# An RWKV-7 group inverse built from squares of 32 rows, with ScalarE copying the results of its last two levels

## The reference, cut to what matters

```
def wkv7_scan(r, w, k, v, a, b):        # a = -kk, b = kk * a
    # state S [64, 64] per head, one step for each token t:
    #   S_t = S_{t-1} * w_t + (S_{t-1} a_t) b_t^T + v_t k_t^T
    #   y_t = S_t r_t
```

## Time and profile before

| | us |
|---|---|
| median of 3 runs | 2042.83 (2038.61 to 2046.37) |
| the profiled execution | 2042.8 |
| its span in the trace | 2041.0 |
| four groups of the inverse (first fill of group 0 to last record of group 3) | 348.2 to 523.8 |
| a group with work of both neighbours beside it (392 to 438, 438 to 484) | 46.0 each |

### The profile page before, as it was taken

One profiled execution on the slowest core, in us unless ns is written; L12 is line 12 of the kernel. 1 busy time (PEld: TensorE's weight loads), 2 busy tenths in 40 slices (PEclk: granted clock), 3 DMA queues, 4 the chain that ended last, 5 costly groups with the idle time before them and its releaser, 6 DMA issues.

```text
span 2041.0 us, 44235 instructions
## 1 busy us (share of the span) xinstructions
PE 1972.0 (97%) x17620; PEld 1877.6 (92%) x17620; DVE 1070.7 (52%) x1648; ACT 922.3 (45%) x1618; POOL 1283.6 (63%) x528
## 2 busy tenths in 40 slices
PE   8999998999999999999998999999999999999998
PEld 8999787788799999999996899999998988999998
DVE  5781577666568734882277487212182345334431
ACT  5333553111243344333447544444456656656553
POOL 6888363000178887888750588877666665677886
PEclk9999999999899999999998999999999999999999
DMA  7445332000044554445430354554445433354552
GB/s 286 167 166 187 125 122 83 3 3 2 9 178 167 183 186 147 183 170 182 162 127 1 121 189 175 196 186 166 145 165 202 150 124 117 135 184 147 185 191 95
DMA packets 40985, 291.46 MB, mean 143 GB/s; under 512 B 4496, under 2 KB 5776, under 8 KB 5904
## 3 DMA queue, kind: packets, MB, share of 16 engines
q1 hardware_dynamic: 40560, 288.26, 39.2%
q10 hardware_dynamic: 288, 1.18, 0.2%
HBM read 288.38 MB, written 1.05 MB: 142 GB/s over the span
## 4 chain that ended last, share of the span: by engine, by line
PE 30%; issue 27%; POOLq 20%; POOL 19%; ACT 2%; DVE 1%; DMA 0%; DVEq 0%; SPq 0%; ACTq 0%
POOLq L2101 19%; POOL w_low L2097 19%; PE ps L635 9%; PE ps L643 9%; PE ps L639 9%; PE ps L1463 1%; PE ps L1450 1%; PE ps L1440 1%; ACT units L2003 0%; POOLq L2096 0%; DMA X<-x_in 0%; ACT units L1534 0%; DVE units L2123 0%; POOLq L2113 0%; ACT w_high L1534 0%
## 5 line engine op out<-in xcount | busy, mean ns | idle before, releaser
L2097 POOL TENSOR_TENSOR w_low<-wring,w_high 128x1024 fp32r<-128x1024 f32 x524 | 1283.4, 2464 | 740.9 <-ACT w_high L1534 710.8
L635 PE MATMUL ps<-in_high,w_high 128*128 128x256 f32 (+1 forms) x2808 | 811.3, 289 | 12.5 <-POOL w_low L2097 4.4
L643 PE MATMUL ps<-in_high,w_low 128*128 128x256 f32 (+1 forms) x2808 | 802.6, 286 | 0.0
L639 PE MATMUL ps<-in_low,w_high 128*128 128x256 f32 (+1 forms) x2808 | 800.9, 285 | 0.0
L1534 ACT ACTIVATE w_high<-wring 128x1024 fp32r<-128x1024 f32 x524 | 542.4, 1055 | 248.5 <-PE ps L635 243.0
L635 PEld LDWEIGHTS ps<-in_high,w_high 128*128 128x128 f32 x2808 | 532.1, 189 | 23.8 <-issue 14.7
L643 PEld LDWEIGHTS ps<-in_high,w_low 128*128 128x128 f32 x2808 | 532.6, 190 | 0.0
L639 PEld LDWEIGHTS ps<-in_low,w_high 128*128 128x128 f32 x2808 | 531.5, 189 | 0.4
L635 PE MATMUL ps<-hid_high,w_high 128*128 128x272 f32 (+1 forms) x880 | 250.6, 285 | 0.0
L643 PE MATMUL ps<-hid_high,w_low 128*128 128x272 f32 (+1 forms) x880 | 250.5, 285 | 0.0
L639 PE MATMUL ps<-hid_low,w_high 128*128 128x272 f32 (+1 forms) x880 | 250.0, 284 | 0.0
(11 more groups left out here) (353 smaller groups left out, 2593.1 us busy)
## 6 DMA issues: line engine op xcount, KB each, us to landing
wring<-stream SPq DMA_DIRECT2D x270, 1024.0 KB, 4.8
con<-consts SPq DMA_DIRECT2D x1, 2199.0 KB, 16.5
X<-x_in SPq DMA_DIRECT2D x1, 1088.0 KB, 8.1
units<-decay ACTq DMA_DIRECT2D x1, 1024.0 KB, 5.2
out<-AL SPq DMA_DIRECT2D x4, 256.0 KB, 2.2
AL<-stream SPq DMA_DIRECT2D x2, 256.0 KB, 20.3
par<-params SPq DMA_DIRECT2D x1, 187.0 KB, 5.9
con<-consts ACTq DMA_DIRECT2D x1, 130.0 KB, 6.1
```

Of the source, the lines that this page charges most:

```text
L635: mm = pe.matmul(o, wh, high(k), start=(k == 0), stop=False)
L639: mm = pe.matmul(o, wh, low(k), start=False, stop=False)
L643: mm = pe.matmul(o, wl, high(k), start=False, stop=(k == kt - 1))
L2097: pool.tensor_tensor(w_low[:, (half + h) % SPLIT_RING, :], wring[:, slot, h * HALF * P:(h + 1) * HALF * P], w_high[:, (half + h) % SPLIT_R ...
```

## The change

The diagonal squares become 32 rows: a chunk of 128 rows is four squares on four partition quarters (`FOURTH`). Levels 0 to 4 are done in the four squares, each with 32x32 matmuls, sixteen per under step where there were eight, on tiles with 128 columns over the four heads where there were 256. Level 5 joins squares 0 and 1 to `FIRST`/`SECOND` halves of the upper square of 64 rows, and squares 2 and 3 likewise, with matmuls beside the diagonal and without a mask; level 6 is as before. The levels 5 and 6 leave VectorE. ScalarE first copies the squares into `rk_joined`, `rk_upper` and `rk_lower` (`rk_assemble`, six copies for each chunk), then copies the results of both levels (`rk_copy_under`, `rk_copy_merge`). The zeros of those tiles are written once, by ten memsets of VectorE at the start of group 0; four memsets in `rk_begin` go. `rk_spread` is cut in two, with the last copies between, and TensorE's variance goes from step 30 to step 32 of the group. The mask constants are smaller.

```diff
@@ -36,6 +36,7 @@
 HALF_ROWS = 64
+BLOCK = 32
@@ -316,9 +317,11 @@
-        RK_SIDE = [min(C, HALF_ROWS) for _, C in CHUNKS]
+        RK_SIDE = [min(C, BLOCK) for _, C in CHUNKS]
...
+        FOURTH = [slice(b, b + BLOCK) for b in range(0, P, BLOCK)]
+        FIRST, SECOND = slice(0, BLOCK), slice(BLOCK, HALF_ROWS)
@@ -874,10 +879,14 @@
                for q in range(4):
                     if n == LEVELS - 1:
-                        mm = pe.matmul(o[BOTTOM, q, :], lb[TOP, q, 0, BOTTOM], x[TOP, q, :], start=True, stop=True)
+                        mm = pe.matmul(o[BOTTOM, q, :], lb[TOP, q, 0, BOTTOM], rk_joined[c][TOP, q, :], start=True, stop=True)
+                    elif n == LEVELS - 2:
+                        for b, below in (FOURTH[0:2], FOURTH[2:4]):
+                            mm = pe.matmul(o[below, q, :], lb[b, q, 0, below], x[b, q, :], start=True, stop=True)
@@ -894,14 +903,20 @@
+                if n == LEVELS - 1:
+                    ot = rk_level_bank(c, 2, HALF_ROWS)
                 for q in range(4):
                     if n == LEVELS - 1:
-                        mm = pe.matmul(ot[TOP, q, :], y[BOTTOM, q, :], rk_lower[g % 2][c][BOTTOM, q, :],
+                        mm = pe.matmul(ot[TOP, q, :], rk_below[c][BOTTOM, q, :], rk_lower[g % 2][c][BOTTOM, q, :],
                                        start=True, stop=True)
                         continue
+                    if n == LEVELS - 2:
+                        pe.matmul(o[FOURTH[1], q, :], xt[FOURTH[1], q, :], y[FOURTH[1], q, :], start=True, stop=True)
+                        for b, below in (FOURTH[0:2], FOURTH[2:4]):
+                            mm = pe.matmul(ot[b, q, :], y[below, q, :], xt[below, q, :], start=True, stop=True)
+                        continue
                     for b in RK_BLOCKS[c] if n < nl - 1 else ():
-                        if n < LEVELS - 2 or b == TOP:
-                            pe.matmul(o[b, q, :], xt[b, q, :], y[b, q, :], start=True, stop=True)
+                        pe.matmul(o[b, q, :], xt[b, q, :], y[b, q, :], start=True, stop=True)
@@ -1056,7 +1071,7 @@
                     rk_mean(before)
-                    yield 30
+                    yield 32
                     rk_variance(before)
@@ -1722,14 +1737,51 @@
+            def rk_assemble(g, c):
+                x, xt, upper, lower = rk_x[c], rk_xt[g % 2][c], rk_upper[g % 2][c], rk_lower[g % 2][c]
+                act.wait_ge(S[f"rk_x{c}_added"], g * RK_COUNT[c] + 8)
+                copy(rk_joined[c][FOURTH[0], :, FIRST], x[FOURTH[0], :, :])
+                copy(rk_joined[c][FOURTH[1], :, SECOND], x[FOURTH[1], :, :])
+                copy(upper[FOURTH[0], :, FIRST], xt[FOURTH[0], :, :])
+                copy(upper[FOURTH[1], :, SECOND], xt[FOURTH[1], :, :])
+                copy(lower[FOURTH[2], :, FIRST], xt[FOURTH[2], :, :])
+                copy(lower[FOURTH[3], :, SECOND], xt[FOURTH[3], :, :])
+            def rk_copy_under(g, c, n):
+                act.wait_ge(S[f"rk_under{c}_ready"], g * RK_LEVELS[c] + n + 1)
+                if n == LEVELS - 1:
+                    ins = copy(rk_below[c][BOTTOM, :, :], rk_level_bank(c, 0, HALF_ROWS)[BOTTOM, :, :])
+                else:
+                    ins = copy(rk_ym[c], rk_level_bank(c, 0))
+                ins.then_inc(S[f"rk_under{c}_masked"], 1)
+            def rk_copy_merge(g, c, n):
+                upper, lower = rk_upper[g % 2][c], rk_lower[g % 2][c]
+                act.wait_ge(S[f"rk_merge{c}_ready"], g * (RK_LEVELS[c] - 1) + n)
+                if n == LEVELS - 1:
+                    copy(lower[TOP, :, :], rk_level_bank(c, 2, HALF_ROWS)[TOP, :, :]).then_inc(S[f"rk_x{c}_added"], 1)
+                    return
+                o, ot = rk_level_bank(c, 1), rk_level_bank(c, 2)
+                copy(rk_joined[c][FOURTH[1], :, FIRST], o[FOURTH[1], :, :]).then_inc(S[f"rk_x{c}_added"], 1)
+                copy(lower[FOURTH[2], :, SECOND], ot[FOURTH[2], :, :])
+                copy(upper[FOURTH[0], :, SECOND], ot[FOURTH[0], :, :]).then_inc(S[f"rk_x{c}_added"], 1)
@@ -1836,8 +1888,20 @@
+                for c in (1, 2):
+                    rk_assemble(g, c)
+                for c in (1, 2):
+                    rk_copy_under(g, c, LEVELS - 2)
+                for c in (1, 2):
+                    rk_copy_merge(g, c, LEVELS - 2)
+                for c in (1, 2):
+                    rk_copy_under(g, c, LEVELS - 1)
                 if g:
-                    rk_spread(g - 1)
+                    rk_squares(g - 1)
+                for c in (1, 2):
+                    rk_copy_merge(g, c, LEVELS - 1)
+                if g:
+                    rk_roots(g - 1)
@@ -2407,44 +2472,34 @@
-                if c and g < 2:
-                    dve.memset(rk_upper[g][c][BOTTOM, :, :], 0.0)
...
+                    if n >= LEVELS - 2:
+                        for c in (*chunks, *chunks):
+                            yield
+                        continue
...
-                        if n == LEVELS - 1:
-                            ins = dve.tensor_copy(lower[c][TOP, :, :], ot[TOP, :, :])
-                        elif n == LEVELS - 2:
-                            tt(rk_x[c][TOP, :, :], o[TOP, :, :], rk_x[c][TOP, :, :], ALU.add
-                               ).then_inc(S[f"rk_x{c}_added"], 1)
-                            tt(upper[c][TOP, :, :], ot[TOP, :, :], xt[c][TOP, :, :], ALU.add)
-                            ins = tt(lower[c][BOTTOM, :, :], ot[BOTTOM, :, :], xt[c][BOTTOM, :, :], ALU.add)
-                        else:
-                            if n < RK_LEVELS[c] - 1:
-                                tt(rk_x[c][0:C, :, :], o, rk_x[c][0:C, :, :], ALU.add).then_inc(S[f"rk_x{c}_added"], 1)
-                            ins = tt(xt[c][0:C, :, :], ot, xt[c][0:C, :, :], ALU.add)
-                        ins.then_inc(S[f"rk_x{c}_added"], 1)
+                        if n < RK_LEVELS[c] - 1:
+                            tt(rk_x[c][0:C, :, :], o, rk_x[c][0:C, :, :], ALU.add).then_inc(S[f"rk_x{c}_added"], 1)
+                        tt(xt[c][0:C, :, :], ot, xt[c][0:C, :, :], ALU.add).then_inc(S[f"rk_x{c}_added"], 1)
@@ -2505,6 +2560,12 @@
+                    yield 0
+                    for c in (1, 2):
+                        dve.memset(rk_joined[c][TOP, :, :], 0.0)
+                        for n in range(2):
+                            dve.memset(rk_upper[n][c], 0.0)
+                            dve.memset(rk_lower[n][c][BOTTOM, :, :], 0.0)
```

More of the change, by code:

```diff
@@ L151 @@
 for _n, _s in (("ident", (P,)), ("ones", (P,)), ("eps", (4,)), ("head_ones", (P,)), ("rope_swap", (P,)), ("ret_swap", (P,)),
-               ("level", (LEVELS - 1, HALF_ROWS)), ("level_0t", (HALF_ROWS,)), ("eye", (HALF_ROWS,)), ("tri", (2, P)), ("reset", (T,)), ("cos", (T,)), ("sin", (T,)),
+               ("level", (LEVELS - 2, BLOCK)), ("level_0t", (BLOCK,)), ("eye", (BLOCK,)), ("tri", (2, P)), ("reset", (T,)), ("cos", (T,)), ("sin", (T,)),
                ("ret_cos", (SEQ,)), ("ret_sin", (SEQ,)), ("causal", (3, T)), ("neg", (3, T)),
@@ L174, in constants @@
                 c[name][base + d, base + half + d] = 1
-    for n in range(LEVELS - 1):
+    for n in range(LEVELS - 2):
         m = 1 << n
-        t, s = r[:, None] % HALF_ROWS, r[None, :HALF_ROWS]
+        t, s = r[:, None] % BLOCK, r[None, :BLOCK]
         c["level"][:, n] = (t // (2 * m) == s // (2 * m)) & (t // m % 2 == 1) & (s // m % 2 == 0)
-    c["level_0t"][:] = np.tile(c["level"][:HALF_ROWS, 0].T, (2, 1))
-    c["eye"][:] = np.tile(np.eye(HALF_ROWS), (2, 1))
+    c["level_0t"][:] = np.tile(c["level"][:BLOCK, 0].T, (4, 1))
+    c["eye"][:] = np.tile(np.eye(BLOCK), (4, 1))
     c["tri"][:, 0] = r[:, None] < r[None, :]
@@ L338, in build @@
         even = carve(group, *[(6, P)] * 3, *[(4, 2, C) for C in sizes] * 2,
-                     *[(4, B) for B in RK_SIDE] * 2, *[(4, HALF_ROWS)] * 4, (6, P))
+                     *[(4, B) for B in RK_SIDE] * 2, *[(4, HALF_ROWS)] * 4, (6, P),
+                     *[(4, HALF_ROWS)] * 2)
         beside_levels = carve(in_parts, *[(4, B) for B in RK_SIDE] * 2, (2, T), (2, T), (4, HD), (4, HD), *[(4, 2, N_META)] * 2,
-                              *[(4, HALF_ROWS)] * 4)
+                              *[(4, HALF_ROWS)] * 4, *[(4, HALF_ROWS)] * 2)
         odd = [carve(flat(v), *shapes) for v, shapes in (
@@ L1847, in _ @@
                     high_parts_to(first + c + 1)
-            rk_spread(3)
+            rk_squares(3)
+            rk_roots(3)
             rk_high(6, 7)
@@ L2425, in rk_levels @@
                         dve.wait_ge(S[f"rk_under{c}_ready"], g * RK_LEVELS[c] + (n + 1))
[L2426 to L2430 removed]
+                        tt(rk_ym[c][0:C, :, :], rk_level_bank(c, 0), tokens_of(level[0:C, n, 0:B], 4), ALU.mult
+                           ).then_inc(S[f"rk_under{c}_masked"], 1)
                         yield
```

18 lines of the change are left out of this document (8 added, 10 removed).

## The result

| | us | |
|---|---|---|
| before | 2044.6 | median of 4 runs, 2038.6 to 2046.6 |
| after | 2064.9 | median of 4 runs, 2058.0 to 2076.3 |
| ratio | 1.0108 | 95% interval 1.0064 to 1.0151 |

The account below looks back on a forecast made before the run. TensorE's list of matmuls was taken to bound the middle groups, VectorE second. Group gains of 3.6, 4.7, 5.4 and 4.8 us make 18.5, less 1.5 for the clock leaves 17: from 2042.8 to 2025 us, range 2010 to 2046.

Parts of the forecast that it names:

- The matmuls: Levels 0 to 5 on TensorE: 832 records four at once, 6.0 us for 12.5; with level 5, 7.7 us less a group.
- two at once: Rival: tiles overlap in pairs only, TensorE gains level 5 alone, 1.2 us a group; 2039 to 2043 us; chance 0.15.
- a floor for every record: Rival: each record costs 0.027 us on any tile, levels 0 to 4 take 22.5 us; 2072 us, slower; chance 0.12.
- VectorE: Masks and additions in the groups: narrower in levels 1 to 4, gone in levels 5 and 6; 8.5 us lighter a group.
- ScalarE: 24 new copies a group, 0.27 us each; 0.6 us charged, last group's merge 1.2 late, root 0.5, table load 0.7.
- The ScalarE rival: Copies between partition quarters cost 0.38 us, TensorE waits 2 to 3 us in each group; 2034 us; chance 0.07.
- The memsets: Ten ahead of group 0's first mask, 2.7 us; group 0 starts 1.3 us later, 2.0 us of matmul gain lost there.
- The clock: Allowance for one more fall of TensorE's granted clock, like the 10.2 us one behind the last group: 1.5 us.
- The rest of the sum: Gains of the four groups after waits: 3.6, 4.7, 5.4 and 4.8 us, together 18.5 before the clock allowance.
- The rival "the clock": Shorter bursts and more waiting bring two falls of the granted clock, each costing up to 5 us; 2034 us; chance 0.08.

Follow-up runs that it names:

- with the clock held: Three unread 128x128 matmuls per under and merge step of both large chunks, added to the kernel before (2120.2 us) and to the changed kernel (2092.7 us).
- wide_four: Changed kernel, memsets moved to steps 10 and 17; levels 1 to 4 stream all heads from q on, up to 128 columns: 2048.7 us, ratio 1.0024.
- first bench: Kernel before, 20 unread matmuls behind the groups replaced by streams: 32x32 on four tiles, 64x64 on two and one, 32x32 on two, 16x16; no time given.
- wide_two: Changed kernel, memsets moved to steps 10 and 17; levels 1 to 4 stream up to two heads, 64 columns: 2047.5 us, ratio 1.0027.
- mixed streams (a) and (b): Kernel before, streams at 545 us: bursts of 64 small 32x32 records on four tiles with 8 or 2 large records between; no network time.

## Why the prediction was wrong, point by point

- **The matmuls: right.** Four tiles do run side by side. The 32 records start 0.0085 us apart (forecast 0.0072), so 832 cost 7.1 us and not 6.0. TensorE's list was to be 7.7 us shorter a group; with the clock held it is 30.4 / 4 = 7.6. The rivals "two at once" and "a floor for every record" fall.
- **VectorE: right in kind.** Its work in the window goes from 111.0 to 84.2 us, 6.7 a group for 8.5 forecast; masks and additions take 0.28 (0.27 assumed).
- **ScalarE: right in size.** Its rows in 345 to 540 us, beside the earlier trace rows:

```profile
L1549 ACT ACTIVATE group<-group 32x128 f32<-32x128 f32 x32 | 9.8, 308 | 5.5 <-DVE in_parts L2188 3.1 <-DVE group L2188 2.0
...
L1549 ACT ACTIVATE in_parts<-ps 64x256 f32<-64x256 f32 x12 | 4.4, 377 | 9.8 <-PE ps L886 9.5 <-PE ps L910 0.2
...
L1549 ACT ACTIVATE group<-ps 32x128 f32<-32x128 f32 x16 | 4.3, 267 | 3.6 <-PE ps L916 3.3
```

  And what TensorE waits for on it, 345 to 560 us (total, times, longest):

```profile
PE ps L960 <- ACT in_parts L1748: 1.0, 1, 1.0
...
PE ps L910 <- ACT in_parts L1549: 0.8, 3, 0.3
```

  `rk_assemble` takes 12 x 0.308 = 3.7 us (3.2, within 2.5 to 4.6). In 345 to 560 us TensorE waits for the new copies 0.8 us at the level-6 merge, in three waits, and 0.3 at the others (0.6 a group was charged, 1.2 in the last), and once 1.0 us for the late root (three times 0.5, and 0.7 for the table load, were charged). The ScalarE rival falls, and with the copies on VectorE the kernel takes 12 us more. With the clock at 1.00 the waits for the copies are longer; wide_four, 340 to 545 us, has 2.7 us of them, with 3.0 charged:

```profile
PE ps L915 <- ACT in_parts L1552: 1.6, 2, 1.3
PE ps L911 <- ACT in_parts L1552: 1.1, 4, 0.3
```

- **The memsets: too small.** The waits view, TensorE, 345 to 395 us (total, times, longest), and the timeline there, for the earlier trace rows:

```profile
PE ps L919 <- DVE in_parts L2188: 6.2, 3, 5.1
PE ps L864 <- DVE group L2188: 2.4, 2, 1.3
PE ps L895 <- DVE group L2188: 2.0, 2, 1.2
```
```profile
354.82 0.93 PE L893 MATMUL ps<-group 32*32 32x32 f32 x69
360.82 0.33 PE L919 MATMUL ps<-in_parts,group 32*32 32x32 f32 x8 [5.06 <-DVE in_parts L2188]
360.95 0.31 PE L921 MATMUL ps<-group,in_parts 32*32 32x32 f32 x8
```

  A wait of 2 to 4 us was forecast, it is 5.06, and the first merge comes 4.3 us later than before. The ten memsets stand in VectorE's timeline from 353.68 to 357.13, 3.45 us for the 2.7 assumed. I charged 1.3 for the start of group 0 and 2.0 for the gain that can't be used there. Moving the memsets away gives 6.0 us in the window and 7.7 on the median, part of which may be the clock; the intervals of the two ratios overlap.
- **The clock: the step that failed.** It reads: "One more such fall somewhere would cost up to half of 10.2; I allow 1.5." There were 99 us more at half clock between 340 and 570, worth up to half of that, 49 us; in the window alone it cost TensorE an estimated 34 us, where 1.5 were allowed. The rest of the sum held: it put 30.8 us of matmuls against 12.3 us of waits and came to 18.5 gained, and the runs show 30.4 against 11.1 us more idle time, 19.3. That the waits agree so well is in part luck, since the memsets took more than their charge and ScalarE's links less. The rival "the clock" had the right mechanism and the wrong price, 10 us.
- **Why it was mis-sized.** I took a fall as one event that follows a wait, because the two in this part of the trace (3.4 us from 346, 10.2 from 526.9) stand behind one each. The streams show that small matmuls alone can bring the low clock about and keep it up, and the wider operands show that it goes when they stream more columns. A hint was in the rows: after the fall at 526.9 TensorE was busy 10.20 of 10.20 us and still at half clock. And four tiles at once, the very thing that I found to be right, makes the thin work no thicker: it ends sooner, and the wait behind it stays. (That last is argued, no run tests it alone.)
- **Small slips in the sums.** 2042.8 less 17 is 2025.8 and not 2025, and the floor's 31 us lost would be 2074 and not 2072. Neither changes a chance.

## What to carry to other kernels

Before cutting matmuls into smaller tiles, ask what it may do to the granted clock of the stretch, and don't take a busy TensorE for an answer: here streams of small tiles with few moving columns ran at 1.2 GHz while it was busy, and the work around them paid with it. Test such a change once with the same unread work in both versions, so that the clock is held; the difference tells whether the code or the clock is at fault. If it is the clock, widening the moving operand can bring it back without another instruction, at the price of the columns; here the price was as high as what the smaller tiles had gained.

## What the runs showed of the hardware that was not expected

- A stream of 16x16 records, TensorE busy all the time, falls to 1.2 GHz; 32x32 on four tiles holds 2.4 GHz with 128 moving columns and not with 32; 128 rows by 32 columns with 32 moving holds it, 32 rows by 128 columns doesn't. The last two differ in shape and in pace (a record every 0.032 and every 0.210 us); which of the two matters is open.
- Records on four tiles start 0.0085 us apart only in bursts. In a long stream TensorE stops after each 128 records, with nothing to wait for ("issue"). The timeline of the first bench, from its fourth microsecond:

```profile
579.52 1.42 PE L1194 MATMUL ps<-con 32*32 32x32 f32 x128 [2.31 <-issue]
582.97 1.93 PE L1194 MATMUL ps<-con 32*32 32x32 f32 x128 [2.03 <-issue]
586.43 1.93 PE L1194 MATMUL ps<-con 32*32 32x32 f32 x128 [1.53 <-issue]
```

  Over the whole stream 3360 records take 89.6 us, 0.0267 each, though four tiles are free. The Trainium skill, "TensorE: Matmul & The Clock Gate", section "Back-to-back issue gap", has about 25 ns as the least from start to start: the runs agree for a long stream and not for a burst. In the groups of after a record comes every 188.9 / 4890 = 0.039 us in the mean, so such stops are fewer there. But they are there, 5.5 us in eight stops from 345 to 560 us, the largest entry this one, where the kernel before has none:

```profile
PE ps L919 <- issue: 2.3, 3, 1.7
```

  They make up half of the 11.1 us more idle time. With wider operands there are fewer (wide_two 4.3 us, wide_four 1.9), so in the kernel their part in the falls can't be told from that of the columns; the dense streams above fell without them.
- The mixed streams (a) and (b) differ only in 8 against 2 records of 128x128 between the same bursts: the first holds 1.00, the second is at 0.50.
